# Mixture-of-experts blocks of 48 rows in place of 64, and expert weights read in runs of 8192 bytes

## The chip, the cores and the metric

One Trainium2 chip, of which the kernel uses one core. The metric is device time in microseconds (us) from launch to end; a profiled execution also gives a span, from the first to the last instruction. TensorE is called PE, its weight loads PEld, VectorE DVE, ScalarE ACT, GpSimd POOL, SyncE SP. TensorE's full clock is 2.4 GHz, and the profile gives the granted clock as a share of it.

## What is computed

A float32 network of two parts, batch 1 and 512 tokens of width 1024. The first part is two attention-like mixer layers with gates. The second prepends 16 meta tokens, and its two layers are a forgetting attention and a recurrence, each followed by a mixture of experts. The change touches only the mixture of experts, cut here to what matters:

```python
g_gate, g_idx = lax.top_k(softmax(xt @ w_grp + b_grp), 1)         # one of 4 groups
e_logit = (xt @ w_rt + b_rt) of the 8 experts of that group
e_val, e_idx = lax.top_k(e_logit, 2)                              # two experts a token
gate = softmax(e_val) * g_gate
expert = g_idx * 8 + e_idx                                        # 0 to 31
a, u = split(x[rows of e] @ w_up[e])                              # w_up[e]: 1024 x 1024
y = (silu(a) * u) @ w_down[e]                                     # w_down[e]: 512 x 1024
h = h + sum over the two experts of gate * y
```

All arithmetic is float32. An expert's weights are 4 MiB (up) and 2 MiB (down), so the 32 experts of a layer have 201.3 MB, all of which are read from HBM in each of the two layers. The first mixture of experts (layer 0) takes 528 tokens in five tiles; the second (layer 1) takes only the 512 tokens in four tiles, since the meta tokens are dropped at the output. For the inputs that the reference draws (its default seed), the largest number of assignments of any one expert is 45 in layer 0; in layer 1 three experts have 54, 54 and 53, and all others 47 or fewer.

## The kernel before, in words

Each mixture of experts runs in three stages.

`stage_route` (L2653) normalises the rows, turns them, computes logits, picks two experts a token and gives each of a token's two assignments a row (slot) of a table of 64-row blocks: block e holds the first 64 rows of expert e, and whatever an expert has beyond 64 goes to overflow blocks 32 and up. SP first issues four small loads of the router's weights and biases (L2625 to L2628) and then the weights of the first experts (`first_three`): up weights 0, down 0, up 1, down 1, up 2. PE waits for the router's loads before it computes logits.

`stage_experts` (L2935) works on pairs of experts. For a pair, DVE builds a 0/1 matrix of tokens by 128 slots (`match`, L2960, and `join`, L2966), PE multiplies the token rows by it (`pick`, L2971: 8 column blocks of the width by 4 or 5 token tiles), which gives the transposed rows of both blocks, and DVE moves them out of PSUM times the norm gain (`place`, L2976). For each expert PE then does the up product (L2982; 8 k-chunks, two halves of the columns), ACT a silu and DVE a product (`act_`), PE four 64-column turns of it (L2987), ACT a copy (L3122), PE the down product (L2994), DVE a copy to `y` (L3196), and ACT issues two stores of the block's rows, 2048 bytes a row each, to `y_rows` (L2999, L3000). The picks of the next pair are spread between: after the up product of an expert come two column blocks, then the hidden turns, then two more. PE's program order is thus up, two picks, turns, two picks, down. Three buffers hold up weights, two hold down weights; SP reloads an up buffer when PE has finished the up product that read it (L2600), and a down buffer after the down product (L2603). Each load is one DMA of 2 MiB, and its contiguous runs are one row of weights, 4096 bytes. The loop is a hardware loop over the first 30 experts, and `last_pair` is written out.

After expert 31 every engine but POOL enters `each` (L3006): it reads the number of overflow blocks and, when this is over zero, walks a hardware loop over all possible blocks (`OVER`), with the body run only where j < count. A body does everything for one block, with nothing prefetched: SP waits for the semaphore `done`, issues the two up loads and the down load; DVE matches and joins; PE picks all eight column blocks, waits for both placings and both up loads, does the up product, and so on; ACT stores the result, waits until the stores have landed, and raises `done` for the next block. Nothing of block j+1 starts before that.

Then POOL gathers each token's two result rows from `y_rows` (L3248), and DVE adds them (L3324, L3382); after layer 1 the sums are the output.

`zero_expert_rows` (L319) zeroes the overflow blocks' rows once, during the attention stage.

## Time and profile before

| | us |
|---|---|
| median of 3 runs | 2815.74 (2813.85 to 2818.06) |
| profiled execution, its own time | 2807.85 |
| its span | 2806.0 |

| engine | busy us | share of the span |
|---|---|---|
| PE | 2567.0 | 91% |
| PEld | 1356.2 | 48% |
| DVE | 875.4 | 31% |
| ACT | 568.4 | 20% |
| POOL | 480.3 | 17% |

In the slices of the profile the 16 DMA engines are busy for 90% or more in two stretches, about 1330 to 1800 us and 2310 to 2740 us: these are the two mixtures of experts. An engine's row "waited for" says who released it at the end of its idle time. A DMA's row gives the time from issue to landing, in which it may lie behind others in the queue. The matrix products are float32 and each is recorded as two MATMUL and two LDWEIGHTS.

### The profile page before, as it was taken

To read this page: it belongs to the slowest core of one execution; us is meant where nothing else is said; L and a number is where in the kernel's file an instruction comes from. 1 tells how busy PE (TensorE), PEld (TensorE's weight loads), DVE (VectorE), ACT (ScalarE), POOL (GpSimd) and SP (SyncE) were. 2 spreads that over 40 slices of the span, in tenths; PEclk is the share of its full clock that TensorE was granted. 3 is DMA by queue.
4 is the path that set the end of the run, shared out by engine and by line. 5 is a ranking of instruction groups with operands and counts; after the bars stand their busy time and mean duration, and the time that the engine had idled before them with its cause. 6 is when DMAs were issued, how large, how long until landed. Compare 5 with 4: busy or idle time off the path is not lost. (4 is left out here: it accounts for less than half of the span.)

```text
span 2806.0 us, 37484 instructions
## 1 busy us (share of the span) xinstructions
PE 2567.0 (91%) x15258; PEld 1356.2 (48%) x15258; DVE 875.4 (31%) x1809; ACT 568.4 (20%) x1341; POOL 480.3 (17%) x682
## 2 busy tenths in 40 slices
PE   7997898988989999889999999959999899989985
PEld 4654444435554454555555555434455454444442
DVE  2306512353251221664111211120556542111112
ACT  2106112232221111631000010021345111000000
POOL 2623210071231121340000000020344200000001
PEclk9998999997999999999999999979999899999997
DMA  5211013110021420125999999951001089999997
GB/s 177 85 66 46 30 35 120 42 41 2 4 77 37 144 90 32 38 77 209 358 411 411 411 411 411 369 193 53 32 32 61 1 337 411 411 411 411 411 411 282
DMA packets 180273, 532.33 MB, mean 190 GB/s; under 512 B 21360, under 2 KB 31472, under 8 KB 180144
## 3 DMA queue, kind: packets, MB, share of 16 engines
q1 hardware_dynamic: 167536, 505.22, 46.5%
q10 hardware_dynamic: 10240, 16.79, 1.6%
q0 software_dynamic: 2368, 8.52, 0.9%
q8 instruction: 91, 1.49, 0.2%
q14 instruction: 38, 0.31, 0.0%
HBM read 507.26 MB, written 23.10 MB: 189 GB/s over the span
## 5 line engine op out<-in xcount | busy, mean ns | idle before, releaser
L344 PE MATMUL psum<-weight_ring,hidden_T 128*128 128x512 f32 (+2 forms) x1216 | 475.9, 548 | 2.7 <-PEq L576 1.6
L344 PEld LDWEIGHTS psum<-weight_ring,hidden_T 128*128 128x128 f32 x1216 | 228.7, 191 | 223.0 <-issue 158.2
L2982 PE MATMUL psum<-arena,hidden_T 128*64 128x512 f32 x1344 | 296.2, 592 | 0.0
L2971 PEld LDWEIGHTS psum<-hidden_T,arena 128*128 128x128 f32 x2304 | 266.8, 192 | 49.6 <-issue 49.6
L2971 PE MATMUL psum<-hidden_T,arena 128*128 128x128 f32 x2304 | 283.3, 278 | 0.0
L2994 PE MATMUL psum<-weight_ring,hidden_T 128*64 128x512 f32 x1024 | 235.4, 602 | 34.1 <-DMA weight_ring<-in_moe_w_down 30.0
L3248 POOL DMA_INDIRECT arena<-expert_rows_out,arena x18 | 20.4, 1133 | 1061.9 <-issue 534.3
L2982 PEld LDWEIGHTS psum<-arena,hidden_T 128*64 128x64 f32 x1344 | 100.5, 137 | 186.9 <-issue 186.9
L2982 PE MATMUL psum<-weight_ring,hidden_T 128*64 128x512 f32 x704 | 155.0, 592 | 0.0
L2994 PEld LDWEIGHTS psum<-weight_ring,hidden_T 128*64 128x64 f32 x1024 | 71.0, 137 | 153.0 <-issue 128.5
L2976 DVE TENSOR_TENSOR hidden_T<-psum,norm_gains 128x512 f32<-128x512 f32 x64 | 44.3, 691 | 293.9 <-PE psum L2982 182.7
L3118 ACT ACTIVATE hidden_T<-psum 128x256 f32<-128x256 f32 x64 | 24.6, 384 | 535.6 <-PE psum L2982 535.6
L344 PE MATMUL psum<-hidden_T,weight_ring 128*128 128x512 f32 (+2 forms) x288 | 123.0, 584 | 3.5 <-PEq L229 1.8
L3494 PE MATMUL psum<-weight_ring,hidden_T 128*128 128x512 f32 x256 | 123.5, 612 | 0.0
L3486 PE MATMUL psum<-hidden_T,weight_ring 128*128 128x512 f32 x256 | 113.0, 601 | 3.7 <-ACT arena L3656 1.7
L2982 PEld LDWEIGHTS psum<-weight_ring,hidden_T 128*64 128x64 f32 x704 | 52.7, 137 | 97.3 <-issue 97.1
L334 POOL TENSOR_TENSOR arena<-arena,constants 128x1 f32<-128x1 f32 (+6 forms) x90 | 98.2, 1091 | 7.5
L330 POOL TENSOR_SCALAR arena<-arena 128x1 f32<-128x1 f32 (+6 forms) x90 | 22.8, 253 | 413.2 <-DVE arena L2336 101.2
L435 PE MATMUL psum<-arena 128*128 128x512 f32 x208 | 91.1, 593 | 0.1
L3118 ACT ACT_TABLE_LOAD x30 | 38.5, 1283 | 242.9 <-issue 226.5
L3183 DVE TENSOR_TENSOR hidden_T<-hidden_T,psum 128x256 f32<-128x256 f32 x60 | 24.9, 415 | 196.7 <-ACT hidden_T L3118 196.7
L344 PEld LDWEIGHTS psum<-hidden_T,weight_ring 128*128 128x128 f32 (+1 forms) x288 | 50.5, 183 | 67.5 <-issue 67.5
(546 smaller groups left out, 3195.5 us busy)
## 6 DMA issues: line engine op xcount, KB each, us to landing
arena<-in_moe_w_up SPq DMA_DIRECT2D x84, 2048.0 KB, 24.1
weight_ring<-in_moe_w_down SPq DMA_DIRECT2D x64, 2048.0 KB, 24.0
weight_ring<-in_moe_w_up SPq DMA_DIRECT2D x44, 2048.0 KB, 23.4
weight_ring<-in_hg_w_in SPq DMA_DIRECT2D x8, 2048.0 KB, 10.6
weight_ring<-in_ev_w_in SPq DMA_DIRECT2D x8, 1536.0 KB, 6.9
weight_ring<-in_fox_w_in SPq DMA_DIRECT2D x6, 2048.0 KB, 8.1
weight_ring<-in_od_w_in SPq DMA_DIRECT2D x5, 2048.0 KB, 8.0
weight_ring<-in_ple_w_gate SPq DMA_DIRECT2D x4, 2048.0 KB, 9.3
```

Of the source, the lines that this page charges most:

```text
L330: g.nc.gpsimd.tensor_scalar(out, sums, scale, EPS, ALU.mult, ALU.add).then_inc(*chain.up())
L334: g.nc.gpsimd.tensor_tensor(out, out, power, ALU.pow).then_inc(*done.up())
L344: last = nc.tensor.matmul(out, l, r, start=i == 0, stop=i == len(left) - 1)
L435: last = nc.tensor.matmul(where[n](p), a[:, k, :], b[:, k, :], start=k == 0 and n in (1, 5, 6), stop=k == 3, skip_group_check=n in (2, 3, ...
L2971: last = nc.tensor.matmul(g.psum[:, c // 4, (c % 4) * P:(c % 4 + 1) * P], keep[:, i, c * P:(c + 1) * P], row[:, i, :], start=i == 0, stop= ...
L2976: return nc.vector.tensor_tensor(xT[:, a, :, :], g.psum[:, a, :].rearrange("p (k r) -> p k r", k=4), gain[:, 4 * a:4 * a + 4].unsqueeze(2) ...
L2982: last = nc.tensor.matmul(g.psum[64 * q:64 * q + 64, 2 + n, :].rearrange("p (s c) -> p s c", s=2), xT[:, k // 4, k % 4, ROWS * n:ROWS * n ...
L2994: last = nc.tensor.matmul(g.psum[64 * q:64 * q + 64, 6 + n, :], aT[:, k % 2, 64 * (k // 2):64 * (k // 2) + 64], down[b][:, k, 512 * q:512 ...
L3118: nc.scalar.activation(s, g.psum[:, 2 + n, 0:256], ACT.Silu).then_inc(silu.sem, 1)
L3183: nc.vector.tensor_tensor(act_, s, g.psum[:, 2 + n, 256:512], ALU.mult).then_inc(hid.sem, 1)
L3486: last = mm(bank(u % 2), w[:, k, (x % 4) * P:(x % 4 + 1) * P], g.hT[:, k, META:], **flags)
L3494: last = mm(bank(u % 2), g.hT[:, k, a:a + n], w[:, k, :], **flags)
```

## The change

Blocks have 48 rows in place of 64 and a pair's matrix has 96 columns in place of 128. The table has 22 overflow blocks in place of 16. An expert with more than 48 assignments now uses an overflow block, where before it took more than 64. The up and down weights are read with two neighbouring rows of the matrix in one partition: each contiguous run is 8192 bytes. So that the k-chunks match, `pick` takes every second column of the token rows as its stationary operand, the hidden turns every second column of `act_`, and the norm gain of this stage is loaded once more in that order with four DMAs of single 4-byte elements (`load_gain`), on SP between the router's loads and the first weights; PE's wait for the router's loads now covers these too. The up product still loads 64 stationary columns, of which the last 16 are another expert's rows or zeros (a memset, once a layer, with a wait on DVE); only 48 rows are stored.

```diff
-ROWS = 64
-OVER = 16
+ROWS = 48
+PAIR = 2 * ROWS
+OVER = 22
+BLOCKS = 11
-    c["steps"] = np.tile(ROWS * np.arange(1, 9, dtype=np.float64), (P, 1))
+    c["steps"] = np.tile(ROWS * np.arange(1, BLOCKS, dtype=np.float64), (P, 1))
...
-    rows = g.a["y_rows"][NEXP * ROWS:].rearrange("(p n) (two c) -> p (n two) c", p=P, c=512)
-    sp.dma_start(rows, zeros.to_broadcast([P, OVER * ROWS // P * 2, 512])).then_inc(*g.y_rows_zeroed.up(16))
+    rows = g.a["y_rows"][NEXP * ROWS:].rearrange("(p n) (two c) -> p (n two) c", p=PAIR, c=512)
+    sp.dma_start(rows, zeros[0:PAIR].to_broadcast([PAIR, OVER * ROWS // PAIR * 2, 512])).then_inc(*g.y_rows_zeroed.up(16))
...
+        self.gain = g.take(4, 2)
+        self.gains = g.a["norm_gains"][:, (4 + layer) * KD:(5 + layer) * KD].rearrange("p (k two) -> p k two", two=2)
+
+    def load_gain(self, sp, loaded):
+
+        for side in range(2):
+            for j in range(2):
+                sp.dma_start(self.gain[64 * side:64 * side + 64, :, j], self.gains[j::2, :, side], allow_slow_non_contiguous=True).then_inc(*loaded.up(16))
 
     def load_up(self, sp, e, n, half):
-        return sp.dma_start(self.up[n][:, 4 * half:4 * half + 4, :], self.wu[bass.ds(e, 1)].rearrange("a (two k p) f -> two p (a k) f", two=2, p=P)[half])
+        return sp.dma_start(self.up[n][:, 4 * half:4 * half + 4, :].rearrange("p (k j) f -> p k (j f)", j=2), self.wu[bass.ds(e, 1)].rearrange("a (two k p j) f -> two p (a k) (j f)", two=2, p=P, j=2)[half])
 
     def load_down(self, sp, e, n):
-        return sp.dma_start(self.down[n], self.wd[bass.ds(e, 1)].rearrange("a (k p) f -> p (a k) f", p=P))
+        return sp.dma_start(self.down[n].rearrange("p (k j) f -> p k (j f)", j=2), self.wd[bass.ds(e, 1)].rearrange("a (k p j) f -> p (a k) (j f)", p=P, j=2))
...
             router.load(sp)
+            weights.load_gain(sp, router.loaded)
             weights.first_three(sp)
...
-            pe.wait_ge(*loaded.at(64))
+            pe.wait_ge(*loaded.at(128))
...
     def pick(cs):
         for c in cs:
             for i in range(T):
-                last = nc.tensor.matmul(g.psum[:, c // 4, (c % 4) * P:(c % 4 + 1) * P], keep[:, i, c * P:(c + 1) * P], row[:, i, :], start=i == 0, stop=i == T - 1)
+                last = nc.tensor.matmul(g.psum[:, c // 4, (c % 4) * P:(c % 4) * P + PAIR], keep[:, i, c // 2 * 2 * P + c % 2:(c // 2 + 1) * 2 * P:2], row[:, i, :], start=i == 0, stop=i == T - 1)
...
-                last = nc.tensor.matmul(..., xT[:, k // 4, k % 4, ROWS * n:ROWS * n + ROWS], wv[:, k, q, :, :], start=k == 0, stop=k == KD - 1)
+                last = nc.tensor.matmul(..., xT[:, k // 4, k % 4, ROWS * n:ROWS * n + 64], wv[:, k, q, :, :], start=k == 0, stop=k == KD - 1)
...
-            last = nc.tensor.transpose(g.psum[:, 4, j * P:(j + 1) * P], act_[:, j * P:(j + 1) * P], g.c("identity"))
+            last = nc.tensor.transpose(g.psum[:, 4, j * P:(j + 1) * P], act_[:, j::2], g.c("identity"))
...
-        a = eng.dma_start(rows[:, 0:512], y[n][0:64, :])
-        b = eng.dma_start(rows[:, 512:], y[n][64:128, :])
+        a = eng.dma_start(rows[:, 0:512], y[n][0:ROWS, :])
+        b = eng.dma_start(rows[:, 512:], y[n][64:64 + ROWS, :])
...
             gates_and_overflow(dve, late)
+            nc.vector.memset(xT[:, :, :, PAIR:PAIR + 16], 0.0).then_inc(*late.up())
+            dve.wait_ge(*late.last())
```

## Rows read from the trace of the kernel before

**Rows 1.** The page: DMA issues (tile, queue, count, KB each, median us to landing).

```profile
arena<-in_moe_w_up SPq DMA_DIRECT2D x84, 2048.0 KB, 24.1
weight_ring<-in_moe_w_down SPq DMA_DIRECT2D x64, 2048.0 KB, 24.0
weight_ring<-in_moe_w_up SPq DMA_DIRECT2D x44, 2048.0 KB, 23.4
```

**Rows 2.** Windows (length, busy PE, PEld, DVE, ACT, POOL, clock, DMA share, GB/s).

```profile
1310.00:1326.00 16.00, 15.66 (x62) 8.20 (x63) 12.38 (x46) 1.43 (x5) 0.00 (x0) 1.00 1.03 410
1856.00:1868.00 12.00, 10.32 (x28) 6.31 (x29) 2.58 (x4) 2.31 (x2) 0.44 (x2) 0.64 1.05 387
2600.00:2700.00 100.00, 90.21 (x521) 48.34 (x519) 17.88 (x34) 8.84 (x16) 0.00 (x0) 1.00 1.03 411
```

**Rows 3.** Who waited for whom, layer 0, 1360 to 1780 us (total, times, longest).

```profile
PE psum L2994 <- DMA weight_ring<-in_moe_w_down: 1.1, 2, 0.6
```

**Rows 4.** Timeline of one expert of layer 0 (start, us, engine, line, operation, count).

```profile
1503.20 3.65 PE L2994 MATMUL psum<-weight_ring,hidden_T 128*64 128x512 f32 x16
1506.68 7.04 PE L2982 MATMUL psum<-arena,hidden_T 128*64 128x512 f32 x32
...
1513.65 2.31 PEld L2971 LDWEIGHTS psum<-hidden_T,arena 128*128 128x128 f32 x20 [0.81 <-issue]
1518.53 3.65 PE L2994 MATMUL psum<-weight_ring,hidden_T 128*64 128x512 f32 x16
```

**Rows 5.** Layer 1: who waited for whom, 2290 to 2780 us.

```profile
PE psum L2994 <- DMA weight_ring<-in_moe_w_down: 27.8, 20, 1.5
```

**Rows 6.** SP's timeline in layer 1 before the queue is full: two reloads of up weights.

```profile
2339.87 0.94 SPq L2600 DMA_DIRECT2D weight_ring<-in_moe_w_up  x2
...
2354.31 0.94 SPq L2600 DMA_DIRECT2D arena<-in_moe_w_up  x2
```

**Rows 7.** Timeline of layer 1: a later down product, and the last that waits.

```profile
2508.79 3.65 PE L2994 MATMUL psum<-weight_ring,hidden_T 128*64 128x512 f32 x16 [1.35 <-DMA weight_ring<-in_moe_w_down]
...
2748.15 3.65 PE L2994 MATMUL psum<-weight_ring,hidden_T 128*64 128x512 f32 x16 [1.52 <-DMA weight_ring<-in_moe_w_down]
```

**Rows 8.** DMA queues, window 4 to 5 us, while constants of 7704 bytes a partition load.

```profile
DMA packets 54, 0.42 MB, mean 416 GB/s; under 512 B 0, under 2 KB 0, under 8 KB 54
```

**Rows 9.** Timeline elsewhere: weight loads of 128 columns before matmuls of one moving column.

```profile
497.56 0.97 PEld L1219 LDWEIGHTS psum<-constants,arena 128*128 128x128 f32 x8 [4.62 <-issue]
```

**Rows 10.** SP's timeline at the start of layer 1, and PE's first logits.

```profile
2250.96 0.43 SPq L2628 DMA_DIRECT2D arena<-in_moe_b_rt  x1
...
2257.08 1.07 PE L2719 MATMUL psum<-hidden_T,arena 128*36 128x128 f32 x16
```

**Rows 11.** Timeline of the end of layer 1's experts.

```profile
2766.52 0.42 DVE L3205 TENSOR_TENSOR hidden_T<-hidden_T,psum 128x256 f32<-128x256 f32 x1 [6.97 <-ACT hidden_T L3118]
...
2769.42 0.44 PE L2987 MATMUL psum<-constants,hidden_T 128*128 128x128 f32 x2
...
2777.29 0.69 DVE L3209 COPY arena<-psum 128x512 f32<-128x512 f32 x1 [7.06 <-PE psum L2994]
2778.01 0.47 ACTq L2999 DMA_DIRECT2D expert_rows_out<-arena  x1
...
2784.06 0.95 POOL L3248 DMA_INDIRECT arena<-expert_rows_out,arena  x1 [0.30 <-issue]
```

**Rows 12.** The page: DMA issues on a queue that is nearly empty, and the expert stores.

```profile
weight_ring<-in_ev_w_out SPq DMA_DIRECT2D x2, 2048.0 KB, 7.8
forget_gate_rows<-arena SPq DMA_DIRECT2D x1, 33.0 KB, 1.6
expert_rows_out<-arena ACTq DMA_DIRECT2D x64, 128.0 KB, 5.8
```

**Rows 13.** Windows of PE alone, after it had been idle from 1292.6 us (busy, clock, DMA).

```profile
1296.00:1298.00 2.00, 0.25 (x3) 0.50 0.59 121
1304.00:1306.00 2.00, 2.00 (x22) 0.81 1.03 424
```

More of the change, by code:

```diff
@@ L2945, in stage_experts @@
     turned, placed = (turned0, turned1), (placed0, placed1)
-    gain = g.gain(4 + layer)
+    gain = weights.gain.rearrange("p k j -> p (k j)")
     up, down = weights.up, weights.down
@@ L2950, in stage_experts @@
     xT = flat[:, 0:2 * 512].rearrange("p (a k r) -> p a k r", a=2, k=4)
-    row, match0, match1 = (flat[:, 1024 + 640 * n:1024 + 640 * n + T * P].rearrange("p (t r) -> p t r", t=T) for n in range(3))
+    row, match0, match1 = (flat[:, 1024 + 640 * n:1024 + 640 * n + T * PAIR].rearrange("p (t r) -> p t r", t=T) for n in range(3))
     s, act_, aT = flat[:, 2944:3200], flat[:, 3200:3456], flat[:, 3456:3712].rearrange("p (j r) -> p j r", j=2)
@@ L2955, in stage_experts @@
     yr = g.a["y_rows"]
-    numbers = g.c("slots").unsqueeze(1).to_broadcast([P, T, P])
-    of = [slot[:, k, 0:T].unsqueeze(2).to_broadcast([P, T, P]) for k in range(2)]
+    numbers = g.c("slots")[:, 0:PAIR].unsqueeze(1).to_broadcast([P, T, PAIR])
+    of = [slot[:, k, 0:T].unsqueeze(2).to_broadcast([P, T, PAIR]) for k in range(2)]
     def match(k, out):
@@ L2981, in tensor_up @@
             for q in range(2):
-                last = nc.tensor.matmul(g.psum[64 * q:64 * q + 64, 2 + n, :].rearrange("p (s c) -> p s c", s=2), xT[:, k // 4, k % 4, ROWS * n:ROWS * n + ROWS], wv[:, k, q, :, :], start=k == 0, stop=k == KD - 1)
+                last = nc.tensor.matmul(g.psum[64 * q:64 * q + 64, 2 + n, :].rearrange("p (s c) -> p s c", s=2), xT[:, k // 4, k % 4, ROWS * n:ROWS * n + 64], wv[:, k, q, :, :], start=k == 0, stop=k == KD - 1)
         return last
```

8 lines of the change are left out of this document (4 added, 4 removed).

## The prediction

> **What bounds the kernel now.** I read the page first: DMA issues by tile, and the slices, which show two stretches with full DMA engines. Then windows inside these, the waits of each, the timeline of one expert in each layer, SP's issues, and last the end of layer 1.
>
> The page counts 128 up loads and 64 down loads of 2 MiB [rows 1]. That is exactly 64 experts: no overflow block runs today. In both stretches the DMA engines move 410 to 411 GB/s at a share of 1.03 [rows 2], so they are full.
>
> Layer 0 is nevertheless set by PE. From one down product to the next it takes 1518.53 - 1503.20 = 15.33 us an expert [rows 4], with PE never idle; it waited for DMA only 1.1 us in 28 experts [rows 3]. One expert moves 6.291 MB of weights and 0.262 MB of results, 15.95 us at 411 GB/s, which is more than 15.33. PE lives on the two to three experts that were prefetched while it routed, and the stage ends just as this lead is used up.
>
> Layer 1 has four token tiles and its PE pace is shorter: 2354.31 - 2339.87 = 14.44 us [rows 6]. Its lead is soon gone, and from then on an expert takes (2748.15 - 2508.79) / 15 = 15.96 us, 15 experts lying between these two down products, with DMA waits before them [rows 7], 27.8 us of them in 20 waits [rows 5]. That is the 15.95 us of the bytes. So layer 1 is bound by DMA up to the last wait at 2748.15 [rows 7]; the rest is a fixed chain.
>
> **Part 1: 48 rows in the matrices.** The pick's moving operand shrinks from 128 to 96 columns. Twenty loads of 128 stationary columns take 2.31 us [rows 4], and less the last's own 0.19 us this is 0.112 us each. Eight loads before matmuls of one moving column take 0.97 us [rows 9], again (0.97 - 0.19) / 7 = 0.111 us. The spacing is that of the weight load, whatever streams. So the narrower pick gains nothing. The up product still streams 512 columns per 64 loaded ones, and the down product too: 0 us. DVE's match, join and place run over a quarter fewer elements, but beside PE; only at the start of a layer are they on the path. I take 0.4 us gained in layer 0, none in layer 1, where DMA decides.
>
> **Part 2: every second column as stationary operand.** No row shows a strided stationary read. Below, a gain is excluded, since the same number of columns is loaded. Above, I take a doubled load, 0.112 us more for each of the 44 loads (40 of the pick, 4 of the turns) of a layer-0 expert. I take 0, as the nearest row is the same load with contiguous columns; the other end is a rival. The Trainium skill (SBUF - State Buffer, the note on cachelines under the DMA port map) lets four fp32 stride for free as long as two accesses hit each 16-byte line, and a stride of two does this; no run shows it yet.
>
> **Part 3: fewer stored bytes.** A block stores 196,608 bytes in place of 262,144. Over the 29 experts before the last wait that is 1.90 MB, in runs of 2048 bytes, for which the rate is 387 GB/s [rows 2]: 4.9 us in layer 1. In layer 0 PE hides it.
>
> **Part 4: runs of 8192 bytes.** Loads with 2048-byte runs go at 387 GB/s, with 4096-byte runs at 410 [rows 2]. Per engine that is 84.7 and 159.8 ns a run, thus 75.1 ns for 2048 bytes and 9.6 ns a run on top. Run on in a straight line, 8192 bytes take 310 ns, or 423 GB/s. The constants, 7704 bytes a partition, were moved as packets of 7.8 KB, so long runs aren't cut, but at 416 GB/s in a window of only 1 us [rows 8]. Ends: 410 (no gain) and 423; I take 420. Up to layer 1's last wait 31 ups and 30 downs are read, 192.9 MB: 470.5 us at 410, 459.3 at 420, so 11.2 us saved. With part 3 it is 16.1 us. Of that about 1.0 is given back: the prefetch of 16.8 MB ends 1.0 us earlier, and SP then idles until a buffer is free. An expert's bytes would take 15.49 us, still over PE's 14.44, so DMA remains the bound. In layer 0 PE's 15.33 stays the bound and only the 1.1 us of waits goes.
>
> The Trainium skill (DMA: Bandwidth & Descriptors, Why small descriptors are slow) counts a fixed 3 cycles a packet beside 128 cycles for 4096 bytes. By that rule the rate would rise from 410 only by 131/128 over 259/256, to 415, and the time would be about 5 us above my forecast; the 9.6 ns from the rows are larger than such an overhead.
>
> **Part 5: the gain's loads.** Four more DMAs stand on SP before the first weights. The last bias load took SP 0.43 us [rows 10], so 4 x 0.45 = 1.8 us; their 1024 four-byte pieces may hold the queue for up to 1.7 us more. I take 2.5 us, all of it lost in layer 1 (ends 1.8 and 3.5). In layer 0 it comes out of the prefetch's lead, which the shorter traffic makes up. PE's first logits are at 2257.08 and the loads would be issued by 2251.4 + 1.8 = 2253.2 [rows 10] and land about 2 us later, so the wider wait costs nothing. The memset and its wait on DVE lie beside the first pick: 0; without that cover some 0.3 us. Zeroing 1056 rows in place of 1024 lies under attention: 0.
>
> Layer 1 thus gains 16.1 - 1.0 - 2.5 = 12.6 us (ends 2 and 17), layer 0 gains 1.5 us.
>
> **Part 6: overflow blocks run.** This decides. Counting the reference's own assignments, layer 0 has 45 at most, below 48. Layer 1 has three experts above 48 (54, 54, 53): three blocks that didn't run before, one after another, nothing prefetched. One block, from `done`:
> - Loads: two up loads land at about 0.5 + 4.19 MB / 420 + 2.4 = 12.9 us. The 2.4 is what 7.8 us leaves above 2.10 MB at 387 GB/s [rows 12].
> - Beside it: matching and joining, 2.0 us; then 64 pick loads. PE has been idle for about 5 us by then. After such an idle stretch PE ran at a granted clock of 0.50, that is 1.2 GHz, and was back towards 2.4 GHz some 7 us after its restart [rows 13]. At half clock a load takes twice 0.112. With 5 us at half: 22 picks, and 42 at full in 4.7 us, so 9.7 us. Two placings, 1.1 us, and hand-overs, 0.3: ready at 13.1, just after the loads.
> - Up product 7.1 us, to 20.2. DVE's product takes 0.4 and the turns 0.4 [rows 11]; silu and copy have as many elements as the product, 0.4 each; with hand-overs of 0.3: 22.1. Down product 3.65: 25.8. Copy 0.7 and two store issues, the first 0.47 us, together 1.1: 27.6 [rows 11]. Landing 2.2 us, between 1.6 for a small store and 5.8 for one in heavy traffic [rows 12]: 29.8. Flags and the loop's own instructions, 1.2: 31.0 us.
> - Ends: with PE at full clock throughout and a landing of 1.6, loads bind and it is 29 us; with half clock throughout and 5.8, 14.3 + 14.1 + 7.3 us of products give 49 us.
>
> Three blocks are 93 us, and entering the first costs perhaps 1.5. Block 1 starts at 2778.0 and the stores of expert 31, which end the stage today, land at about 2781.3, so 3.3 us are shared: 91.2. The loop then walks 19 empty turns. No row shows one; GpSimd's untraced instructions between two gathers take 0.30 us [rows 11], which I take: 5.7 us, with ends of 0 and 1.6 each, if each jump had to fetch code like a small transfer. Together 97 us (ends 84 and 178). After that come the same gathers as now.
>
> **The sum.** -1.5 - 12.6 + 97 = +83 us. The profiled execution took 2807.85 us with a span of 2806.0, so it becomes 2891. It lies 7.9 us below the median of the runs, 2815.74; on the median's scale I predict 2899 us.
>
> **The rivals.**
> 1. *The blocks cost much more.* PE's clock stays at 1.2 GHz through each block, or the empty turns fetch code. For it: half clock lasted 7 us after an idle stretch. Against: two thirds of a block's PE work comes after the first pick. With 130 to 178 us for them the time is 2932 to 2980. Chance 0.12.
> 2. *Strided stationary columns are slow.* Place: each pick. At a doubled load, layer 0's pace becomes 15.33 + 44 x 0.112 = 20.2 us, over 30 experts +147 us. Layer 1's becomes 14.44 + 36 x 0.112 = 18.5, above the 15.96 of now: it costs from 1.5 us an expert on, and gives about +87. With the overflow blocks and their picks (+23) the time is about 3170. Nothing in the trace speaks for it, nothing excludes it. Chance 0.06.
> 3. *No overflow block runs* (the device's counts stay at 48 or below): the change is then only its gains, 2815.7 - 14.1 = 2802 us, faster. Against: 54 and 53 are far from 48, and rounding moves single tokens. Before the change the counts leave no mark in the trace, as all are below 64. Chance 0.05.
> 4. *Long runs bring nothing*: layer 1 gains 2 us or less and the time is 2910. Inside my range; with the forecast, 0.77.
>
> **How the numbers follow.** Forecast with rival 4: 0.77, from 2880 to 2925 by its own bounds. The range of 2870 to 2945 takes in part of rival 1. Rival 2, rival 3 and rival 1's upper part, about 0.17, stay outside. A measurement of this kernel can tell about 0.2%, some 6 us, from no change. Slower by more: 0.93. Faster: 0.05. Between: 0.02.
>
> **What would show it.** In the page, up loads rise by 6 and down loads by 3. After layer 1's last `last_pair` product there are three groups of 64 pick matmuls with about 31 us between them, during which the DMA engines are busy for less than half. Layer 0's pace stays at 15.33 us; layer 1's falls to about 15.5, and GB/s to 418 to 420. A pace above 15.5 in layer 0 would mean the strided load. Wrong would be a count of overflow blocks other than three, or blocks of 40 us.

## The result and the profile after

The changed kernel takes 2890.78 us (2886.33 to 2894.28, 4 runs) against 2816.45 us (2813.85 to 2818.06, 4 runs) of the kernel before, on the same chip: 74.3 us more, a ratio of 1.0264 with a 95% interval of 1.0246 to 1.0282. The forecast was 2899 us in a range of 2870 to 2945, slower: the direction, the range and the cause hold, the closeness in part by luck (see the account of the terms below). The profiled execution took 2894.28 us, with a span of 2892.4, where the span before was 2806.0.

I cut both spans at five events that each trace has: SP's first router load of layer 0, the first gather after layer 0's experts, the first router load of layer 1, the small memset on DVE that stands behind layer 1's last experts, and the next gather.

| stretch (us) | before | after | difference | forecast |
|---|---|---|---|---|
| start to layer 0's router load | 1293.0 | 1296.7 | +3.7 | 0 |
| layer 0's experts | 537.2 | 541.1 | +3.9 | -1.5 |
| between the layers | 419.1 | 421.8 | +2.7 | 0 |
| layer 1's experts | 528.6 | 509.6 | -19.0 | -12.6 |
| overflow loop of layer 1 | 4.8 | 99.4 | +94.6 | +97 |
| rest | 23.3 | 23.9 | +0.6 | 0 |

The +3.7 and +2.7 lie in stages that the change doesn't touch. Over all traces of this study the first stretch took between 1291.1 and 1298.4 us and the third between 418.1 and 421.8; one and the same kernel (56 rows, profiled twice) had 1296.8 and 1291.1 in the first. So a few us in such a stretch say nothing of the change.

Of the changed kernel first the page: DMA issues (tile, queue, count, KB each, median us to landing).

```profile
arena<-in_moe_w_up SPq DMA_DIRECT2D x84, 2048.0 KB, 14.6
weight_ring<-in_moe_w_down SPq DMA_DIRECT2D x67, 2048.0 KB, 13.9
weight_ring<-in_moe_w_up SPq DMA_DIRECT2D x50, 2048.0 KB, 13.6
```

Against [rows 1] these are 6 up loads and 3 down loads more: three overflow blocks ran, as counted. A load lands some 14 us after its issue in place of 24.

The windows of the changed kernel (length, busy PE, PEld, DVE, ACT, POOL, clock, DMA share, GB/s), as in [rows 2]:

```profile
1310.00:1326.00 16.00, 15.62 (x104) 9.71 (x101) 11.94 (x40) 1.29 (x4) 0.00 (x0) 1.00 1.01 423
2600.00:2700.00 100.00, 95.66 (x540) 50.81 (x541) 15.75 (x33) 8.83 (x16) 0.00 (x0) 1.00 1.01 422
```

423 and 422 GB/s stand where 410 and 411 stood. PE's timeline in layer 0, to be laid beside [rows 4]:

```profile
1509.86 3.65 PE L3005 MATMUL psum<-weight_ring,hidden_T 128*64 128x512 f32 x16
...
1520.31 2.43 PEld L2982 LDWEIGHTS psum<-hidden_T,arena 128*128 128x128 f32 x20 [0.81 <-issue]
1522.87 2.45 PEld L2982 LDWEIGHTS psum<-hidden_T,arena 128*128 128x128 f32 x20
1525.41 3.65 PE L3005 MATMUL psum<-weight_ring,hidden_T 128*64 128x512 f32 x16
```

An expert takes 1525.41 - 1509.86 = 15.55 us in place of 15.33. Twenty loads of every second column take 2.43 to 2.45 us in place of 2.31.

Layer 1, who waited for whom from 2290 to 2769 us (total, times, longest):

```profile
PE psum L3005 <- DMA weight_ring<-in_moe_w_down: 6.4, 10, 0.8
```

and SP's up loads of two neighbouring experts there:

```profile
2644.43 1.21 SPq L2610 DMA_DIRECT2D arena<-in_moe_w_up  x2
2659.74 0.90 SPq L2610 DMA_DIRECT2D weight_ring<-in_moe_w_up  x2
```

The waits fell from 27.8 us in 20 [rows 5] to 6.4 in 10, all of them after 2600 us. Until then PE goes at its own pace, 14.61 us an expert, on the weights that were prefetched, while the engines move 422 to 423 GB/s from 2310 us on: as in the kernel before, DMA is full all along and its bytes set when the stage ends. Where PE waits, an expert takes 15.31 us in place of 15.96.

A part of layer 1's 19.0 us has another cause. The last down product, before and then after:

```profile
2771.89 5.35 PE L2994 MATMUL psum<-weight_ring,hidden_T 128*64 128x512 f32 x16 [2.03 <-ACT hidden_T L3122]
```

```profile
2764.81 3.65 PE L3005 MATMUL psum<-weight_ring,hidden_T 128*64 128x512 f32 x16 [1.62 <-ACT hidden_T L3133]
```

Behind its wait of 2.03 us the kernel before did this product at a granted clock that fell to 0.50 (window 2773 to 2775 us) and took 1.7 us more than every other such product of its experts. The wait alone doesn't bring this: in layer 0 the same product, behind the same wait of 2.03 us, took 3.65. So these 1.7 us are the clock's and not the bytes'; whether every execution has them no run here tells.

The timeline of the first overflow block and of the second's start (start, us, engine, line, operation, idle time before and what ended it):

```profile
2769.15 0.06 DVE L3224 MEMSET hidden_T<- 128x1 f32 x1
...
2769.41 0.95 SPq L2610 DMA_DIRECT2D weight_ring<-in_moe_w_up  x2
...
2771.26 9.30 PE L2982 MATMUL psum<-hidden_T,arena 128*128 128x96 f32 x64 [2.80 <-DVE hidden_T L2977]
2780.67 1.02 DVE L2987 TENSOR_TENSOR hidden_T<-psum,arena 128x384 f32<-128x384 f32 x2 [9.39 <-PE psum L2982]
2782.26 8.78 PE L2993 MATMUL psum<-weight_ring,hidden_T 128*64 128x512 f32 x32 [1.70 <-DMA weight_ring<-in_moe_w_up]
...
2798.11 0.33 ACTq L3011 DMA_DIRECT2D expert_rows_out<-hidden_T  x1
2800.11 1.03 DVE L2971 TENSOR_TENSOR hidden_T<-constants,arena 128x384 f32<-128x384 f32 x2 [2.68 <-ACTq L3163]
...
2801.78 10.10 PE L2982 MATMUL psum<-hidden_T,arena 128*128 128x96 f32 x64 [5.09 <-DVE hidden_T L2977]
```

The next block's match stands 2.0 us behind the last store issue: it waits until the stores have landed. The match begins at 2769.59 in the first block, at 2800.11 in the second and at 2829.28 in the third: 30.5 and 29.2 us a block. The end of the third block and the loop's empty turns:

```profile
2857.14 0.32 ACTq L3011 DMA_DIRECT2D expert_rows_out<-hidden_T  x1
2868.54 1.07 POOL L3261 DMA_INDIRECT arena<-expert_rows_out,arena  x1 [603.25 <-PEq L3373]
```

And windows during the first block's picks, and in the up product behind the wait of 1.70 us (columns as above; the clock is the number after POOL's). Of these 1.70 us, 1.26 are the placing, which comes before every block's up product, and 0.44 are DMA's:

```profile
2773.00:2775.00 2.00, 2.00 (x12) 2.00 (x11) 0.00 (x0) 0.00 (x0) 0.00 (x0) 0.50 1.04 434
2777.00:2779.00 2.00, 2.00 (x20) 2.00 (x18) 0.00 (x0) 0.00 (x0) 0.00 (x0) 1.00 1.02 434
2783.00:2785.00 2.00, 2.00 (x8) 0.56 (x6) 0.00 (x0) 0.00 (x0) 0.00 (x0) 0.53 1.01 430
```

### The profile page after: what moved, and what is told of

It reads as the page before. It is cut to its first block and busy times, and to the rows that moved or that the text cites. A ratio compares the mean times of both kernels' runs of the same rounds, so it can differ in the third digit from the quotient of the medians.

```text
span 2892.4 us, 38657 instructions
## 1 busy us (share of the span) xinstructions
PE 2648.7 (92%) x15600; PEld 1408.6 (49%) x15600; DVE 865.3 (30%) x1835; ACT 570.7 (20%) x1347; POOL 479.4 (17%) x682
## 5 line engine op out<-in xcount | busy, mean ns | idle before, releaser
L2982 PEld LDWEIGHTS psum<-hidden_T,arena 128*128 128x128 f32 x2496 | 311.4, 200 | 65.2 <-issue 49.6
L2982 PE MATMUL psum<-hidden_T,arena 128*128 128x96 f32 x2496 | 324.4, 287 | 13.0 <-DVE hidden_T L2977 13.0
L3005 PE MATMUL psum<-weight_ring,hidden_T 128*64 128x512 f32 x1072 | 244.7, 598 | 11.3 <-DMA weight_ring<-in_moe_w_down 6.4
L2993 PE MATMUL psum<-weight_ring,hidden_T 128*64 128x512 f32 x800 | 177.9, 597 | 4.2 <-DVE hidden_T L2987 2.5
L2987 DVE TENSOR_TENSOR hidden_T<-psum,arena 128x384 f32<-128x384 f32 x70 | 38.8, 558 | 335.5 <-PE psum L2993 182.7
L3005 PEld LDWEIGHTS psum<-weight_ring,hidden_T 128*64 128x64 f32 x1072 | 72.3, 136 | 133.4 <-issue 121.7
L2993 PEld LDWEIGHTS psum<-weight_ring,hidden_T 128*64 128x64 f32 x800 | 58.5, 138 | 116.5 <-issue 113.0
## 6 DMA issues: line engine op xcount, KB each, us to landing
weight_ring<-in_hg_w_in SPq DMA_DIRECT2D x8, 2048.0 KB, 10.8
```

Of the source, the lines that this page charges most:

```text
L2982: last = nc.tensor.matmul(g.psum[:, c // 4, (c % 4) * P:(c % 4) * P + PAIR], keep[:, i, c // 2 * 2 * P + c % 2:(c // 2 + 1) * 2 * P:2], ro ...
L2987: return nc.vector.tensor_tensor(xT[:, a, :, 0:PAIR], g.psum[:, a, :].rearrange("p (k r) -> p k r", k=4)[:, :, 0:PAIR], gain[:, 4 * a:4 * ...
L2993: last = nc.tensor.matmul(g.psum[64 * q:64 * q + 64, 2 + n, :].rearrange("p (s c) -> p s c", s=2), xT[:, k // 4, k % 4, ROWS * n:ROWS * n ...
L3005: last = nc.tensor.matmul(g.psum[64 * q:64 * q + 64, 6 + n, :], aT[:, k % 2, 64 * (k // 2):64 * (k // 2) + 64], down[b][:, k, 512 * q:512 ...
```

## The experiments

All ratios are to the kernel before on the same chip. In the diffs "-" is the changed kernel and "+" the experiment, shortened where they say so. The stretches in this section are cut at the same events as in the table above.

### The two halves of the change, each alone

`rows48_only` has 48 rows and all that follows from it, but the loads, operands and gain of the kernel before:

```
 def load_up(self, sp, e, n, half):
-    return sp.dma_start(self.up[n][...].rearrange("p (k j) f -> p k (j f)", j=2), ... "two p (a k) (j f)" ...)
+    return sp.dma_start(self.up[n][...], self.wu[...].rearrange("a (two k p) f -> two p (a k) f", two=2, p=P)[half])
...
-            weights.load_gain(sp, router.loaded)
...
-    ... keep[:, i, c // 2 * 2 * P + c % 2:(c // 2 + 1) * 2 * P:2] ...
+    ... keep[:, i, c * P:(c + 1) * P] ...
```

> Blocks of 48 rows with the runs of 4096 bytes, contiguous stationary operands and no extra gain loads. My theory: layer 0 at 15.33 us an expert as before, layer 1 at 15.8 us in its DMA-bound part (5 us saved on stores), three overflow blocks and 19 empty turns with some 96 us; together about +90 us, 2907 us. Rival for the pick: if fewer moving columns make it faster, layer 0's pace falls below 15.2 us. Rival for the slower pace in the changed kernel's layer 0: if it came from the blocks and not from the stride, it is 15.55 here too.

`runs_only` is the opposite, the changed kernel without the memset and its wait, which only narrower blocks need, and with

```
-ROWS = 48, OVER = 22, BLOCKS = 11
+ROWS = 64, OVER = 16, BLOCKS = 9
```

> Blocks of 64 rows as before; only the 8192-byte runs with what they need: strided stationary operands and the gain's loads. My theory: layer 0 goes from 15.33 to 15.55 us an expert through the strided weight loads alone (the pick has 128 moving columns again, so if the pace is the same as in the changed kernel the narrower pick brought nothing). Layer 1's DMA-bound pace is 14.8 us for the weights at about 425 GB/s plus 0.68 for the stores, 15.5 us, so the stage is 14 us shorter; together -10 us, 2806 us. Rival: the 96-column pick did save PE time and hid part of a dearer strided load; then layer 0's pace here is above 15.7 us.

Measured: `rows48_only` 2898.86 us (2896.46 to 2904.51), ratio 1.0312 (1.0296 to 1.0329); `runs_only` 2806.02 us (2798.44 to 2808.49), ratio 0.9977 (0.9967 to 0.9986).

| stretch (us) | before | rows48_only | runs_only | both (after) |
|---|---|---|---|---|
| layer 0's experts | 537.2 | 533.0 | 544.5 | 541.1 |
| layer 1's experts | 528.6 | 522.5 | 514.5 | 509.6 |
| overflow loop | 4.8 | 103.4 | 4.8 | 99.4 |

So the rows alone save 6.1 us in layer 1 and 4.1 in layer 0, and cost 98.6 in blocks, where I had expected some 96; the long runs save 14.1 us in layer 1 and lose 7.3 in layer 0. The last down product of a layer blurs these sums. In layer 1 it took 5.35 us in the kernel before alone, so 1.7 us of each saving there is its clock: the rows save 4.4 and the runs 12.4, together 16.8 against 19.0 - 1.7 = 17.3. In layer 0 it took 5.35 us in `runs_only` alone, so the runs lose 5.6 there; -4.1 + 5.6 = +1.5 against +3.9. Most of what is missing are the waits for DMA at the end of layer 0, which were 2.2 us before, 0.6 with the rows and none with the runs: both halves take away the same ones.

The overflow loop doesn't add up: the blocks cost 98.6 us with runs of 4096 bytes and 94.6 with 8192. The up products of the first two blocks of `rows48_only` show where the 4.0 us are:

```profile
2784.73 9.23 PE L2992 MATMUL psum<-weight_ring,hidden_T 128*64 128x512 f32 x32 [4.23 <-DMA weight_ring<-in_moe_w_up]
...
2816.36 8.78 PE L2992 MATMUL psum<-weight_ring,hidden_T 128*64 128x512 f32 x32 [2.00 <-DMA weight_ring<-in_moe_w_up]
```

The up loads land 13.1 to 13.5 us after the first of them was issued, in place of 12.3 to 12.9, PE waits 2.0 us or more in each of the three blocks (4.23, 2.00 and 2.08), and each up product then takes 8.6 to 9.2 us in place of 7.09, where the changed kernel has one such product. So the long runs save 4 us in the blocks too, mostly through the clock.

The layer-0 loss goes with the strided operands. In `rows48_only`, which has 96 moving columns as well but contiguous stationary ones, PE shows

```profile
1503.06 2.31 PEld L2981 LDWEIGHTS psum<-hidden_T,arena 128*128 128x128 f32 x20
1505.47 3.65 PE L3004 MATMUL psum<-weight_ring,hidden_T 128*64 128x512 f32 x16
```

thus the same 2.31 us as [rows 4], and its pace is 15.27 us an expert; `runs_only` has 15.58. That is (2.44 - 2.31) / 20 = 0.0065 us a load, and 0.26 us for the 40 picks of an expert, of the 0.28 between 15.55 and 15.27. The other suspect, the 8192-byte writes of the DMA engines beside PE, is ruled out by the loads that stayed contiguous: those of the up product take 137 ns each before, after and in the run with 16384 bytes below, while the picks' go from 192 to 196 and 328 ns.

### 56 rows in place of 48

The largest counts of layer 1 are 54, 54 and 53, so 56 rows hold all of them.

```
-ROWS = 48, OVER = 22, BLOCKS = 11
+ROWS = 56, OVER = 18, BLOCKS = 10
...
-            nc.vector.memset(xT[:, :, :, PAIR:PAIR + 16], 0.0).then_inc(*late.up())
+            nc.vector.memset(xT[:, :, :, PAIR:PAIR + 8], 0.0).then_inc(*late.up())
```

> Blocks of 56 rows (18 overflow blocks possible), all else as in the changed kernel: runs of 8192 bytes, every second column as stationary operand, the gain's four loads. Layer 1's largest expert has 54 rows, so no overflow block should run. My theory: the change lost its time to the three overflow blocks and the empty loop turns (94.6 us between the last memset and the first gather, by its trace), and the rest is a gain. Then: 128 up loads and 64 down loads, no block; layer 0 at 15.55 us an expert (+4 us for the stage), layer 1 at about 15.4 us in its DMA-bound part (stage 17 us shorter); together about 13 us less than before, 2803 us, between 2797 and 2811. Rival: the changed kernel also lost some 6 us in stages that the change doesn't touch (its layer-1 routing began 10.3 us later, only 3.9 of it from layer 0), because moved code or data slows them; then this kernel has them too and stands at 2809 or above.

Measured: 2799.32 us (2796.34 to 2802.56), ratio 0.9955 (0.9941 to 0.9968). The page counts 64 down loads, and the overflow loop takes 4.3 us. The rival, that moved code or data slows stages which the change doesn't touch, had 2809 us or above and is out. With no block to run the rest of the change is a gain of 0.45%: the loss lies in the threshold of 48 against counts of 53 and 54, and not in smaller blocks as such.

### The empty turns

```
-            with eng.Fori(0, OVER) as j:
+            with eng.Fori(0, 3) as j:
```

> The changed kernel, but the loop over possible overflow blocks has 3 turns in place of 22, which is enough for these inputs. My theory: an empty turn costs about 0.36 us. From the issue of the last block's second store to the first gather the changed kernel takes 11.4 us, of which 4.2 were there before; this falls to about 4.5 us, a gain of 7 us. Rival: the time goes into leaving the loop once (a jump that fetches code), and stays at 10 us or more.

Measured: 2883.58 us in one run. Its rows at the end:

```profile
2855.41 0.32 ACTq L3011 DMA_DIRECT2D expert_rows_out<-hidden_T  x1
2858.50 1.07 POOL L3261 DMA_INDIRECT arena<-expert_rows_out,arena  x1 [594.57 <-PEq L3373]
```

From the last store's issue to the gather it is 3.09 us here and 11.40 in the changed kernel: 8.3 us for 19 empty turns, 0.44 each. The forecast had 0.30.

### What sets a block: the picks at half clock, or the loads?

In the changed kernel both end within about a microsecond of each other. PE's picks and placings were through 12.2, 13.0 and 13.7 us after the match of the three blocks, and in all runs in which PE waited for 8192-byte up loads they landed 12.3 to 12.9 us after their first issue, which stands within 0.2 us of the match. Four runs, one of each, pull them apart. The first gives PE work before each block, so that its clock is up when the picks start:

```
             def body(j):
+                keep_busy(nc, g.psum[:, 3, :], g.c("identity"), keep[:, 1, 0:512], 8)
                 pe.wait_ge(oh, j + 1)
```

> The changed kernel, with eight matmuls of 512 columns (about 0.43 us each) on PE in each overflow block before its wait for the match, so that PE's granted clock is near 1.00 when the picks start. In the changed kernel the 64 picks of the three blocks took 9.3, 10.1 and 10.8 us at a clock that began at 0.50; at full clock they would take 64 x 0.112 = 7.2. Theory 1: the picks with their placings and the loads end within about 1 us of each other (block 1's up product waited 1.70 us for DMA after the picks, those of blocks 2 and 3 started as the loads landed, some 13 us after their issue), so faster picks only lengthen the wait for DMA. The block before the first costs 1.7 us less (its up product at full clock, 7.1 in place of 8.8) and the other two at most 0.3 us each: from the memset to the first gather 99.4 - 2 = 97 us, and the waits for DMA before the up products are 2 to 3 us. Theory 2: the picks at half clock bind. Then each block loses 2 to 3.5 us and the stretch is about 91 us, with no wait for DMA of more than 0.5 us.

Measured: 2890.31 us in one run; the overflow loop takes 97.95 us in place of 99.39. The first block and the third's up product:

```profile
2772.94 7.67 PE L2982 MATMUL psum<-hidden_T,arena 128*128 128x96 f32 x64
2781.87 7.09 PE L2993 MATMUL psum<-weight_ring,hidden_T 128*64 128x512 f32 x32 [1.26 <-DVE hidden_T L2987]
...
2839.17 7.09 PE L2993 MATMUL psum<-weight_ring,hidden_T 128*64 128x512 f32 x32 [1.27 <-DMA weight_ring<-in_moe_w_up]
```

The picks take 7.67 us in place of 9.3 to 10.8, yet a block gains 0.5 us on average: in the second and third block DMA ends the wait, 12.6 and 12.4 us after the match began, where PE's own chain had taken 13.0 and 13.7. The waits of 2 to 3 us for DMA that theory 1 wanted didn't come: they are 1.43 and 1.27 us, of which 1.26 are the placing. The eight products ran twice as long as I had meant, 7.13 us, and held the picks back by some 4 us in the first block and 1.8 in the others, so this run doesn't decide. I halved them. The halving also caught a call of the same form in the router, which makes layer 0 2.8 us and layer 1 1.1 us longer in that run; it lies outside the blocks.

```
-                keep_busy(nc, g.psum[:, 3, :], g.c("identity"), keep[:, 1, 0:512], 8)
+                keep_busy(nc, g.psum[:, 3, :], g.c("identity"), keep[:, 1, 0:512], 4)
```

> The changed kernel with half as many products in front of each overflow block's picks as the run before it with eight, whose products (recorded as 16 matmuls of 0.44 us) ran for 7.13 us and held the first block's picks back by 3.5 us. Four take 3.6 us and are through before the match is ready, so the picks start about 2 us after the memset, at full clock, and take 7.7 us; with the placings they end near 11 us after the memset, 2 us before the loads, which land 12.3 to 13.1 us after the match begins. Theory 1: DMA sets the up product's start, so PE waits 1.5 to 3 us for it; in the changed kernel a wait of 1.70 us was followed by an up product of 8.78 us in place of 7.09, at a granted clock of 0.53. So the up products come at 8 to 8.8 us, the picks' gain is given back and the stretch from the memset to the first gather is 97 to 99.5 us, no better than the 98.0 of the run with eight. Theory 2: faster picks shorten the block. Then the stretch falls by the 2 us that the picks were held back in that run, to 92 us or less.

Measured: 2892.40 us in one run; the overflow loop takes 101.13 us, 3.2 more than with eight and 1.7 more than with none. Blocks one and three:

```profile
2769.35 7.67 PE L2982 MATMUL psum<-hidden_T,arena 128*128 128x96 f32 x64
2779.54 8.73 PE L2993 MATMUL psum<-weight_ring,hidden_T 128*64 128x512 f32 x32 [2.53 <-DMA weight_ring<-in_moe_w_up]
...
2829.44 7.78 PE L2982 MATMUL psum<-hidden_T,arena 128*128 128x96 f32 x64 [1.44 <-DVE hidden_T L2977]
2840.49 8.78 PE L2993 MATMUL psum<-weight_ring,hidden_T 128*64 128x512 f32 x32 [3.27 <-DMA weight_ring<-in_moe_w_up]
```

and a window at the start of the first up product:

```profile
2779.00:2781.00 2.00, 1.46 (x4) 0.53 (x6) 0.00 (x0) 0.00 (x0) 0.00 (x0) 0.62 1.02 434
```

Fast picks, at last early, end in a wait of 2.5 to 3.3 us, of which 1.3 to 2.0 are DMA's; behind it PE works at half clock again and the up product takes 1.7 us longer. Faster picks turn into a wait and the wait into a slower product: theory 1, and more of it than the 97 to 99.5 us that I expected. The rows add up to the 1.7 us: against the changed kernel the up products start 0.1, 0.4 and 1.0 us sooner after their match, and the second and the third take 1.7 us longer each. Slow picks in the changed kernel were the cheaper way to spend this time.

The third run takes the loads forward instead: SP waits for the last products that read the buffers, not for the whole block before.

```
-                sp.wait_ge(done, j + 1)
+                sp.wait_ge(ur, j + 1)
...
+                sp.wait_ge(dr, j + 1)
...
+                pe.sem_inc(ur, 1)
+                pe.sem_inc(dr, 1)
```

> The changed kernel, but an overflow block's weights are loaded as soon as the last products that read their buffers are through, in place of after the whole block before: block 1's beside expert 31, the others beside the tail of the block before. PE's clock is left to itself. Theory 1: picks (9.3 to 10.8 us) and loads end together, so alone this brings little: block 1 loses its 1.7 us wait for DMA, blocks 2 and 3 keep their pick chain and lose at most 0.5 us each; from the memset to the first gather 96 to 97.5 us, no waits for DMA before the up products. Theory 2: the loads bind and the picks hide beside them; then each block falls by what the loads are early, some 3 us, and the stretch is about 90 us.

Measured: 2897.40 us in one run, and 107.85 us for the overflow loop, 8.5 more than without. Neither theory had this. The rows between the first and the second block:

```profile
2786.09 0.94 SPq L2610 DMA_DIRECT2D weight_ring<-in_moe_w_up  x2
...
2791.74 0.37 SPq L2613 DMA_DIRECT2D weight_ring<-in_moe_w_down  x1
...
2792.98 0.34 ACTq L3011 DMA_DIRECT2D expert_rows_out<-hidden_T  x1
2799.30 1.03 DVE L2971 TENSOR_TENSOR hidden_T<-constants,arena 128x384 f32<-128x384 f32 x2 [7.00 <-ACTq L3168]
```

The block's stores now share the engines with 6.3 MB of weights that were issued before them. The next match, which waits until they have landed, comes 6.3 and 6.4 us after the last store issue in place of 2.0: 8.8 us in all, against the 8.5. The median time from issue to landing says the same; the stores' row in a window of this run, and in one of the changed kernel:

```profile
expert_rows_out<-hidden_T ACTq DMA_DIRECT2D x2, 96.0 KB, 5.9
```

```profile
expert_rows_out<-hidden_T ACTq DMA_DIRECT2D x2, 96.0 KB, 1.9
```

In full traffic it was 5.8 before, too [rows 12]. The wait for DMA before the first up product is gone, as expected, but the picks before it, left at half clock longer, took 10.67 us in place of 9.30; the net is worth little beside this.

The fourth run has both edits together:

> Both edits: the early loads and the eight matmuls that keep PE's clock up. If picks at half clock and loads hide each other, as theory 1 of the two single edits has it, both together bring more than the sum of each alone: the 64 picks take 7.2 us, the up product 7.1 us without a wait, and a block falls from about 31 and 29 us to 26, the stretch from the memset to the first gather from 99.4 to about 89 us. If one of the two alone bound the blocks, both together bring no more than that one.

Measured: 2895.96 us in one run, 105.94 us for the overflow loop. The first block's picks took 7.67 us with no wait behind them; the second's and third's came so late behind the stores that PE was idle for 2.3 us after its extra work, and took 9.3 us. The expected 89 us was 17 too low. The landing of the stores, which no step of mine had tied to the loads, is 8.5 of them; most of the rest are the first block's picks, which stood 4 us behind the extra products, and picks of 9.3 us in place of 7.2 in the other two. What the order would be worth with a match that doesn't wait for the stores wasn't tried.

### Longer runs still

56 rows, the up weights in runs of 16384 bytes, and every fourth column as the pick's stationary operand:

```
-        return sp.dma_start(self.up[n][...].rearrange("p (k j) f -> p k (j f)", j=2), ... p=P, j=2)[half])
+        return sp.dma_start(self.up[n][...].rearrange("p (k j) f -> p k (j f)", j=4), ... p=P, j=4)[half])
...
-    ... keep[:, i, c // 2 * 2 * P + c % 2:(c // 2 + 1) * 2 * P:2] ...
+    ... keep[:, i, c // 4 * 4 * P + c % 4:(c // 4 + 1) * 4 * P:4] ...
```

> Blocks of 56 rows, so that no overflow block runs, and the up weights read in runs of 16384 bytes, four neighbouring rows a partition (the pick then takes every fourth column as stationary operand); the down weights stay at 8192, and the norm's gain comes by 16 small loads in front. It carries the line through 84.7, 159.8 and 309.9 ns for 2048, 4096 and 8192 bytes further: 9.6 ns a run and 75.1 ns for each 2048 bytes give 609 ns, or 430 GB/s for the up loads and 428 over all. Theory 1 (the fixed time of a run is real): a window of pure up loads goes at 429 to 430 GB/s and the DMA-bound pace of layer 1 falls from 15.30 to 15.1 or 15.2 us an expert of two up loads and one down. Theory 2 (the gain ends at 8192, or pieces are cut there): 423 as with runs of 8192 bytes, no gain. For the stationary operand: a stride of two cost 0.005 us a load. If the cost goes with the stride, a stride of four costs about 0.010 to 0.015 and layer 0's pace is 15.7 to 16.0 us, against 15.55; the Trainium skill (SBUF - State Buffer, the note on cachelines) needs two hits in each line of 16 bytes, of which a stride of four makes one, and by that a load would take longer by much more than that, towards twice. The sixteen gain loads take SP 10.8 us by 0.67 each, and delay the start of each layer's experts by as much.

Measured: 3061.34 us in one run. The window of layer 0's first loads, and PE's loads of twenty picks:

```profile
1310.00:1326.00 16.00, 15.62 (x121) 10.57 (x118) 10.07 (x33) 1.29 (x4) 0.00 (x0) 0.92 1.01 429
```

```profile
1508.18 4.74 PEld L2982 LDWEIGHTS psum<-hidden_T,arena 128*128 128x128 f32 x20
```

The straight line from 84.7 and 159.8 ns goes through 8192 bytes, 309.9 ns at 423 GB/s, and gives 430 GB/s for 16384. The window holds a down load of 8192-byte runs beside the up loads, and the line gives 428 for this mix; 429 was measured, but windows of 16 us in this stage lie between 426 and 429, so 16384 bytes fit the line and don't prove it. Less the last one's own time (0.19, 0.20 and 0.33 us), a load takes 0.112 us with contiguous columns, 0.118 with a stride of two and (4.74 - 0.33) / 19 = 0.232 with a stride of four. Layer 0's experts take 692.3 us in place of the 541.2 of 56 rows with 8192 bytes, and layer 1's 625.3 in place of 513.9, so the pace of 15.1 or 15.2 us that I expected in layer 1 can't be read. The cost doesn't go with the stride in proportion; it is small at two and doubles the load at four. By the Trainium skill (SBUF — State Buffer, the note on cachelines under the DMA port map) an access needs at least two hits in a line of 16 bytes for full speed. A stride of two floats has two and one of four has one, so both rows agree with this, but for the 0.006 us that a stride of two does cost. The same note's distance of four fp32 that are free can't be read as a stride of four: here the measurement decides. My second rival was right in its price; it had the wrong stride.

### Each layer with the loads that suit its bound

56 rows; layer 0 with 4096-byte runs, contiguous operands and no gain loads, layer 1 as in the changed kernel, but with its gain loads behind the first expert's weights:

```
     def load_up(self, sp, e, n, half):
+        if not self.layer:
+            return sp.dma_start(self.up[n][...], self.wu[...].rearrange("a (two k p) f -> two p (a k) f", two=2, p=P)[half])
...
+            if n == 0 and self.layer:
+                self.load_gain(sp, self.gain_in)
```

> Blocks of 56 rows (no overflow block runs) and each layer with the loads that suit what bounds it: layer 0, which PE sets, with runs of 4096 bytes, contiguous stationary columns and no gain loads; layer 1, which DMA sets, with runs of 8192 bytes and every second column, its gain loads issued behind the first expert's weights. Theory 1 (the strided stationary read costs layer 0 0.22 to 0.25 us an expert, and the gain loads 2.7 us of layer 1's DMA time): layer 0's pace is 15.3 us in place of 15.55, layer 1's 15.3 where DMA sets it, and the time is 6.5 + 2.7 = 9 us below that of 56 rows with both layers alike, so 2790 to 2794 us, a ratio of 0.992 to 0.993. Theory 2 (layer 0's slower pace comes from elsewhere, say from DMA writing 8192-byte runs beside it): its pace stays near 15.5 only if the down loads matter too, which are also at 4096 here, so then it would be 15.3 as well; but if the gain loads' time is hidden by the prefetch's lead, only 6.5 us come and the ratio is 0.993 to 0.9945.

> Blocks of 56 rows with runs of 8192 bytes in both layers, again, on the chip of the run by layer and beside it. As before: no overflow block, a ratio of 0.9955, some 9 us more than with the loads chosen by layer if the strided read and the gain loads are what was read from the traces; the same as it if they are not.

Measured, on one chip: by layer 2792.03 us (2791.51 to 2794.67), ratio 0.9938 (0.9925 to 0.9952); 56 rows with both layers alike 2798.37 us (2793.67 to 2801.74), ratio 0.9961 (0.9947 to 0.9975). The 6.3 us between the medians are about what layer 0 alone was expected to give, and not the 9 of both; as the two ranges touch, the stages carry this reading. Layer 0's experts took 536.1 us by layer, with 2.31 us for twenty loads, and 541.2 alike; layer 1's took 513.7 and 513.8. So the gain loads cost nothing. SP's rows by layer, and then alike, show why:

```profile
2249.54 0.37 SPq L2643 DMA_DIRECT2D arena<-in_moe_w_grp  x1
...
2251.67 0.95 SPq L2614 DMA_DIRECT2D weight_ring<-in_moe_w_up  x2
...
2253.17 7.91 SPq L2609 DMA_DIRECT2D arena<-in_norm_gains  x4
...
2296.56 0.95 SPq L2614 DMA_DIRECT2D weight_ring<-in_moe_w_up  x2
```

```profile
2251.25 0.37 SPq L2635 DMA_DIRECT2D arena<-in_moe_w_grp  x1
...
2253.38 2.70 SPq L2607 DMA_DIRECT2D arena<-in_norm_gains  x4
2256.12 1.12 SPq L2610 DMA_DIRECT2D weight_ring<-in_moe_w_up  x2
...
2298.17 0.95 SPq L2610 DMA_DIRECT2D weight_ring<-in_moe_w_up  x2
```

The first weights go out 2.13 us after the router's load in the one and 4.87 in the other. The first reload stands 47.02 and 46.92 us after it, in both: it waits for a buffer that PE frees, and PE's start is set by the routing. A prefetch that starts 2.7 us earlier only ends earlier. By its median this version is the fastest of the study.

## Why the prediction was right, and which terms were off

- **The bounds.** PE in layer 0, DMA in layer 1: held. As DMA's rate rose more than I took, PE's first wait in layer 1 comes after 2600 us, where it came before 2500; the bytes set the end of the stage all the same. The signs that I had named came: six and three loads more, three groups of 64 picks, and a pace above 15.5 in layer 0, which was to mean the strided load. The engines were busy for 56% of the blocks' time and not for less than half.
- **Part 1, narrower picks.** Nothing in the picks' loads, as said: 2.31 us for twenty at 128 and at 96 columns. Layer 0 gained 4.1 us in all where I had 0.4 for the narrower blocks and 1.1 for the waits. Its waits for DMA were 2.2 us in all, as two of them lie behind the window of [rows 3]; 0.6 us of them stayed, and the pace of 15.27 against 15.33 is some 1.8 us over 30 experts.
- **Part 2, strided columns.** The mis-sized term of layer 0. I took 0 between ends of 0 and 0.112 us a load, and it is 0.006. In `runs_only` the pace rose by 0.25 us, 7.5 us over 30 experts, of which the waits for DMA that vanish give back 2.2. In layer 1, where DMA's bytes set the end, it is hidden.
- **Part 3, fewer bytes.** Forecast 4.9 us in layer 1; measured 6.1 alone, of which 1.7 are the clock of the last down product, so 4.4.
- **Part 4, long runs.** The upper end, 423 GB/s, was right, and I had taken 420. The Trainium skill (DMA: Bandwidth & Descriptors, Why small descriptors are slow) would have given an estimate of 415 by its 3 cycles; the measured 423 decides for the 9.6 ns read from the rows. With 423 the part is 192.9 MB at 410 less the same at 423 = 14.5 us, 13.5 with what is given back at the start, and `runs_only` measured 14.1, or 12.4 without the 1.7 of the clock. The long runs also saved 4 us in the blocks, for which I had nothing.
- **Part 5, the gain's loads.** SP took 2.69 us for them, near my 2.5. But that all of it would be lost in layer 1 was the step that failed. I had noted that a prefetch which ends earlier leaves SP idle until a buffer is free, and didn't apply it to the loads in front of that prefetch. Taking the 2.5 out and 423 in gives -18.4 for layer 1; measured -19.0, or -17.3 without the 1.7 us of the clock.
- **Part 6, the blocks.** Three, as counted. The second block, from its match: up product at 13.0 us (forecast 13.1), down product's end at 25.8 (25.8), last store issue's end at 27.5 (27.6), next match at 29.2 (31.0). The work was right to a few tenths; what follows it was 1.8 us shorter, with stores that landed in 1.9 us (2.2) and less for the flags. The first block had a wait of 1.70 us and an up product at half clock, 1.7 us more. The empty turns cost 8.3 us and not 5.7. Together 94.6 against 97: two errors against each other. My ends for this term don't follow from its steps, which give 30.2 and 49.8 us a block and 89 to 178 us for the term, where I wrote 84 to 178; the forecast doesn't hang on them.
- **Luck.** The sum is nearer than its terms. Against the forecast layer 0 came 5.4 us higher, layer 1 6.4 lower, the blocks 86.3 us and not 91.2, the empty turns 2.6 higher. That 80.1 us remain against 83 is errors of 19 us in all that nearly cancel; the range would have held without that.
- **The scale.** The parts of the trace that the change touches give 3.9 - 19.0 + 94.6 + 0.6 = +80.1 us against my +83. That is 3 of the 8 us by which 2899 lies above 2890.8. The rest is the choice of executions: the profiled one of before was 7.9 us below its median, which I added, the profiled one of after 3.5 above its own, and the stretches that the change leaves alone took 6.4 more in it: 2.9 + 7.9 + 3.5 - 6.4 = 7.9 us.
- **The rivals.** Blocks of 40 us and more, no blocks, and no gain from long runs are out by the rows above. The slow strided read came true only at a stride of four.

## What to carry to other kernels

A bound on a data-dependent loop is part of the cost of a tile size: count the data first, since a block that takes one expert too many through a loop with nothing prefetched (30 us here) outweighs what all the smaller tiles save (4 us a layer). Look at what a layout change for DMA does to the operands of the engine that reads it, and give it only to the stage that DMA bounds. And before a transfer is moved forward, look which small transfer of the same moment somebody waits for: here stores of 0.2 MB behind 6.3 MB of weights cost more than the prefetch could give.

## What the runs showed of the hardware that I had not expected

- A run of contiguous bytes from HBM costs each engine about 9.6 ns beside 75.1 ns for each 2048 bytes: 387, 410 and 423 GB/s with runs of 2048, 4096 and 8192 bytes. With up weights at 16384 and down weights at 8192, windows lie at 426 to 429.
- An fp32 weight load of 128 columns takes 0.112 us with contiguous columns, 0.118 with every second and 0.232 with every fourth, one behind the other.
- In the overflow blocks, behind PE's waits of 1.70, 2.53, 3.16 and 3.27 us, the up product took 8.73 to 8.78 us, and the granted clock fell to 0.50 to 0.53 (1.2 GHz) in its first microseconds; behind waits of 1.26 to 1.43 us it took 7.09. The wait alone doesn't settle it: the last down product took 5.35 or 3.65 us behind the same wait of 2.03 us in the kernel before, and behind the same 1.96 us in `runs_only`.
- An empty turn of the loop, which every engine but POOL walks, takes 0.44 us (8.3 us for 19).
- Four loads of single 4-byte elements hold SP for 2.69 us on an empty queue and for 7.91 us behind 6.3 MB of weights.
